# Squares on ScalarE and moved outer products, with attention's first tiles inside the projection and packed scores

## The reference

```
hn   = rmsnorm(x, norm1_g);  proj = hn @ w_in        # 1024 x 2048: q, k, v, u of 512 each
q, k: 4 heads, 2 components of 64;  v: 4 heads of 128
sc   = q . k * 64**-0.5 - slope[h] * |qpos - kpos|   # per head and component
p    = softmax(sc);  a = p[0] - lam * p[1];  att = a @ v
ssm  = bi_s5_glu(u, ...)                             # state space scan, both directions
h    = x + [rmsnorm(att) * 0.2 ; ssm] @ w_out
h    = h + relu(rmsnorm(h) @ w1)**2 @ w2;  y = rmsnorm(h)
```

## Time and profile before

| | |
|---|---|
| median of 3 runs | 2681.01 us (2678.62 to 2682.8) |
| profiled execution, its span | 2681.7 us |
| PE busy | 2562.9 us, 96% |
| DVE busy | 2093.3 us, 78% |
| ACT busy | 1416.5 us, 53% |
| POOL busy | 327.2 us, 12% |
| projection | 0 to about 398 us |
| attention | about 402 to 1006 us |
| state space stage and the rest | 1010 to 2681.7 us |

### The profile page before, as it was taken

One profiled execution on the slowest core, in us unless ns is written; L12 is line 12 of the kernel. 1 busy time (PEld: TensorE's weight loads), 2 busy tenths in 40 slices (PEclk: granted clock), 3 DMA queues, 4 the chain that ended last, 5 costly groups with the idle time before them and its releaser, 6 DMA issues.

```text
span 2681.7 us, 32621 instructions
## 1 busy us (share of the span) xinstructions
PE 2562.9 (96%) x12804; PEld 2155.2 (80%) x12804; DVE 2093.3 (78%) x2074; ACT 1416.5 (53%) x1737; POOL 327.2 (12%) x221
## 2 busy tenths in 40 slices
PE   7998998999999998988989999999999999999998
PEld 5887777999999986766867888888887888888886
DVE  5866638999999976776898877677888886678885
ACT  3276616878787772224444566543334665543334
POOL 6310001101010003320334000000014000000003
PEclk8999998999999999998999999999999999999999
DMA  5356643020204008977565554452234664452221
GB/s 182 111 181 224 221 135 79 25 69 23 72 23 109 24 11 227 267 232 271 186 220 219 220 222 173 173 219 95 94 111 160 247 219 173 173 204 94 94 79 63
DMA packets 162520, 397.17 MB, mean 148 GB/s; under 512 B 29376, under 2 KB 86976, under 8 KB 134592
## 3 DMA queue, kind: packets, MB, share of 16 engines
q1 hardware_dynamic: 145664, 319.06, 35.9%
q10 hardware_dynamic: 16704, 76.03, 7.2%
HBM read 270.79 MB, written 122.16 MB: 147 GB/s over the span
## 4 chain that ended last, share of the span: by engine, by line
PE 44%; DVE 3%; POOL 1%; DMA 1%; issue 1%; ACT 0%; DVEq 0%; SPq 0%; ACTq 0%; POOLq 0%
PE ml_bank L2447 15%; PE ml_bank L2449 15%; PE ml_bank L2448 15%; POOL kp_tabs L2056 1%; DMA kp_low<-hn_s 1%; DVE ml_res L2327 0%; DVE ml_hb L2361 0%; DVE ml_b_split L2258 0%; DVE ml_w_split L2269 0%; DVE ml_res L2347 0%; DVE ml_rinv L2353 0%; PE ml_bank L2455 0%; DMA ml_hb<-h_s 0%; DMA hn_s<-ml_hb 0%; DVE kp_low L2282 0%
## 5 line engine op out<-in xcount | busy, mean ns | idle before, releaser
L2447 PE MATMUL ml_bank<-ml_b_split,ml_w_split 128*128 128x512 f32 x2016 | 788.8, 391 | 10.1 <-issue 9.8
L2448 PE MATMUL ml_bank<-ml_b_split,ml_w_split 128*128 128x512 f32 x2016 | 785.8, 390 | 0.0
L2449 PE MATMUL ml_bank<-ml_b_split,ml_w_split 128*128 128x512 f32 x2016 | 785.7, 390 | 0.0
L2447 PEld LDWEIGHTS ml_bank<-ml_b_split,ml_w_split 128*128 128x128 f32 x2016 | 379.3, 188 | 93.9 <-issue 14.6
L2448 PEld LDWEIGHTS ml_bank<-ml_b_split,ml_w_split 128*128 128x128 f32 x2016 | 379.6, 188 | 79.7 <-issue 1.2
L2449 PEld LDWEIGHTS ml_bank<-ml_b_split,ml_w_split 128*128 128x128 f32 x2016 | 379.4, 188 | 79.2
L2056 POOL TENSOR_TENSOR kp_tabs<-kp_tabs,ml_square 128x512 f32<-128x512 f32 x55 | 144.2, 2622 | 1266.4 <-ACT ml_square L2160 1259.9
L942 ACT ACTIVATE at_e<-at_e,at_neg_top 128x2048 f32<-128x2048 f32 x128 | 256.5, 2004 | 43.8 <-DVE at_neg_top L1027 43.8
L1148 PEld LDWEIGHTS at_pv<-at_v,at_a_t 128*128 128x128 f32 x2048 | 258.3, 192 | 16.4
L2327 DVE TENSOR_TENSOR ml_res<-ml_bank,ml_res 128x2048 f32<-128x2048 f32 x75 | 171.5, 2287 | 118.8 <-PE ml_bank L2449 118.8
L2094 ACT ACTIVATE ml_b_split<-kp_u_t 128x2048 fp32r<-128x2048 f32 x54 | 103.5, 1917 | 298.1 <-PE ml_bank L2449 298.1
(11 more groups left out here) (225 smaller groups left out, 4097.9 us busy)
## 6 DMA issues: line engine op xcount, KB each, us to landing
act_s<-ml_res ACTq DMA_DIRECT2D x32, 1024.0 KB, 4.0
kp_wide<-in_w_stream SPq DMA_DIRECT2D x18, 1024.0 KB, 5.1
kp_bp<-in_w_stream SPq DMA_DIRECT2D x18, 1024.0 KB, 5.5
kp_tabs<-in_w_stream SPq DMA_DIRECT2D x18, 1024.0 KB, 5.9
ml_r<-in_w_stream SPq DMA_DIRECT2D x18, 1024.0 KB, 6.7
tab_s<-kp_tabs ACTq DMA_DIRECT2D x32, 512.0 KB, 2.7
kp_low<-hn_s SPq DMA_DIRECT2D x16, 1024.0 KB, 5.5
kp_u_t<-hn_s SPq DMA_DIRECT2D x16, 1024.0 KB, 4.9
```

What stands on the lines that cost most here:

```text
L2447: pe.matmul(out, w_hi[:, w], b_hi[:, b], start=fresh and kt == 0, stop=False, skip_group_check=True)
L2448: pe.matmul(out, w_hi[:, w], b_lo[:, b], start=False, stop=False, skip_group_check=True)
L2449: last = pe.matmul(out, w_lo[:, w], b_hi[:, b], start=False, stop=kt == 3, skip_group_check=True)
```

## The change

**In the projection.** For the first two tiles of x (`BY_ACT = 2`) ACT takes the squares, one by one between its weight splits and, for the second tile, after the first statistic; POOL only adds them. On PE `stats(0)` stands before group 4 instead of 3. DVE makes the low parts of all eight first weight pieces before it inverts (`invert(0)`), where two came after; ACT splits pieces 6 and 7 ahead of the root. SP loads x's second tile ahead of w's pieces 6 and 7, and `s_bc` behind them. The outer products move from (26, 29, 34, 37, 42, 45, 50, 53) to (26, 29, 32, 35, 41, 44, 49, 52).

**Between projection and attention.** They become one block. Attention's tiles are laid over memory that the projection no longer needs, its PSUM tiles over the eight banks of the projection. Keys are loaded after group 56; then ACT, DVE and POOL make the split keys, the bias and tiles 0 and 1 of q between their work for groups 57 to 63, and PE does the four halves of the scores of tiles 0 and 1 behind groups 60, 61, 62 and 63.

**In attention.** `scores(n, half)` does half the keys for both components: four matmuls of 128 rows with k_hi, then four of 64 rows with k_lo, c = 0 on rows 0 to 63 and c = 1 on rows 64 to 127, alternating. q's halves for c = 1 are swapped for that (low part on rows 0 to 63), k_lo is held once per component, and q's low part is made by POOL. DVE adds c = 0 and c = 1 in turn, the combination is done in two halves, and a transposition waits only for its half. q has two buffers instead of four. The first loads of the next stage are issued one part a tile.

The core of the diff:

```diff
-PREP_OUTERS = (26, 29, 34, 37, 42, 45, 50, 53)
+PREP_OUTERS = (26, 29, 32, 35, 41, 44, 49, 52)
...
+        for x in range(BY_ACT):
+            for k in range(1, KD):
+                pool.wait_ge(squared, KD * x + k + 1)
...
+                pool.tensor_tensor(square_sum[:], square_sum[:], v_out[:, k % 2], ALU.add)\
+                    .then_inc(pool_step if k < KD - 1 else squares_ready, 1)
...
+        split_w(1)
+        squares(0, range(3))
+        split_w(2)
+        squares(0, range(3, 5))
+        for i in range(3, HALF_W):
+            split_w(i)
+            if i < 6:
+                squares(0, range(i + 2, i + 3))
+        stats(0)
+        prep.time_steps(act)
+        squares(1, range(KD))
...
+            if n == NG - 7:
+                prep.all_used(act)
+                attention.k_high(act, 0, range(4))
+            if n == NG - 6:
+                attention.q_high(act, 0)
+                attention.k_high(act, 0, range(4, 8))
...
+            if n == NG - 4:
+                for before in range(NG - 6, NG - 4):
+                    evacuated(pe, before)
+                pe.wait_ge(rms_ready, NTB)
+            if n >= NG - 4:
+                attention.scores(pe, (n - NG + 4) // 2, n % 2)
...
+        for c in range(2):
+            self.wait(pe, self.biased, 4 * n + 2 * half + c - 1)
+            for bank, keys in enumerate(cols):
+                pe.matmul(self.score[:, c, bank * TB:(bank + 1) * TB], self.q_hl[:, n % 2, c], self.k_hi[h % 2][:, c, keys],
+                          start=True, stop=False)
+        for bank, keys in enumerate(cols):
+            for c in range(2):
+                rows = slice(c * DH, (c + 1) * DH)
+                last = pe.matmul(self.score[:, c, bank * TB:(bank + 1) * TB], self.q_hl[rows, n % 2, c],
+                                 self.k_lo[h % 2][rows, keys], start=False, stop=True)
...
+        for n in range(2, NS):
+            a.scores(pe, n, 0)
+            for j in range(2, 4):
+                a.turn(pe, n - 2, j)
+            for j in range(2):
+                a.values(pe, n - 2, j)
+            a.scores(pe, n, 1)
+            for j in range(2, 4):
+                a.values(pe, n - 2, j)
+            for j in range(2):
+                a.turn(pe, n - 1, j)
```

More of the change, by code:

```diff
@@ L301, in sign_matrices @@
         dve.wait_ge(self.bc_loaded, 16)
[L302 removed]
+        dve.wait_ge(self.const_step, 8)
         for i in (1, 2):
@@ new lines, in phase_project, with wait, is_v, qku_index @@
+    block = ctx.enter_context(nc.Block())
+    def wait(eng, sem, value):
+        if value > 0:
+            eng.wait_ge(sem, value)
+    def is_v(n):
+        return n >= SECOND and n % NGROUP < NV
+    def qku_index(n):
+        return n if n < SECOND else SECOND + (n - SECOND) // NGROUP * NV + n % NGROUP - NV
+    def v_index(n):
+        return (n - SECOND) // NGROUP * NV + n % NGROUP
+    def evacuated(eng, n):
+        if n < 0:
+            return
+        if is_v(n):
+            eng.wait_ge(v_evacuated, v_index(n) + 1)
+        else:
+            eng.wait_ge(qku_evacuated, qku_index(n) + 1)
@@ new lines, in fresh_x, with x_freed, w_slot @@
+    def fresh_x(b):
+        return b > 0 and BLOCK_X[b] != BLOCK_X[b - 1]
+    def x_freed(eng, b, k):
+        freed = sum(fresh_x(c) for c in range(b))
+        if k < KD - 1:
+            eng.wait_ge(x_used, freed * (KD - 1) + k + 1)
+        else:
+            eng.wait_ge(group_done, b * NGROUP)
+    w_pieces = w_in.rearrange("(k p) n -> p k n", p=P)
+    x_tiles = x_t.rearrange("(k p) t -> p k t", p=P)
+    def w_slot(i):
+        return slice((i % HALF_W) * P, (i % HALF_W + 1) * P)
+    @block.sync
@@ L779, in phase_attention @@
+    return block, attention
+class Attention:
     NQ = S // P
@@ new lines, in k_high, with k_low @@
+    def k_high(self, act, h, pieces):
+        for i in pieces:
+            c, cols = i // 4, slice(i % 4 * TB, (i % 4 + 1) * TB)
+            if i == 0:
+                act.wait_ge(self.k_loaded, 64 * (h + 1))
+                self.wait(act, self.scores_done, 4 * self.NQ * (h - 1))
+            act.activation(self.k_hi[h % 2][:, c, cols], self.k_raw[:, c, cols], ACT.Copy).then_inc(self.k_hi_ready, 1)
+    def k_low(self, eng, h, i):
+        c, cols = i // 4, slice(i % 4 * TB, (i % 4 + 1) * TB)
+        rows = slice(c * DH, (c + 1) * DH)
+        eng.wait_ge(self.k_hi_ready, 8 * h + i + 1)
+        return eng.tensor_tensor(self.k_lo[h % 2][rows, cols], self.k_raw[rows, c, cols],
+                                 self.k_hi[h % 2][rows, c, cols].bitcast(F32), ALU.subtract)
@@ new lines, in combine, with first_half @@
+    def combine(self, dve, n, half):
+        slot, cols = n % 2, slice(half * self.HALF, (half + 1) * self.HALF)
+        dve.wait_ge(self.coef_step, 2 * n + 2)
+        dve.scalar_tensor_tensor(self.e[:, slot, 0, cols], self.e[:, slot, 1, cols], self.coef[:, 1:2],
+                                 self.e[:, slot, 0, cols], ALU.mult, ALU.add).then_inc(self.combined, 1)
+    def first_half(self, dve, n):
+        for c in range(2):
+            self.add_bias(dve, n, 0, c)
+        self.coefficient(dve, n - 1)
+        self.combine(dve, n - 1, 0)
@@ new lines, in turn, with values @@
+    def turn(self, pe, n, j):
+        if not 0 <= n < self.NS:
+            return
+        if j % 2 == 0:
+            pe.wait_ge(self.combined, 2 * n + j // 2 + 1)
+        self.wait(pe, self.turned_out, 4 * n + j - 1)
+        for i in range(4):
+            kt = 4 * j + i
+            last = pe.transpose(self.turned[:, j % 2, i * P:(i + 1) * P], self.e[:, n % 2, 0, kt * P:(kt + 1) * P], self.ident[:])
+        last.then_inc(self.turned_done, 1)
+    def values(self, pe, n, j):
+        if not 0 <= n < self.NS:
+            return
+        h = n // self.NQ
+        if j == 0:
+            self.wait(pe, self.pv_out, n - 1)
+            if n % self.NQ == 0:
+                pe.wait_ge(self.v_loaded, 64 * (h + 1))
+        pe.wait_ge(self.turned_out, 4 * n + j + 1)
+        for kt in range(4 * j, 4 * j + 4):
+            last = pe.matmul(self.pv[:, n % 2, 0:P], self.a_t[:, n % 2, kt], self.v[h % 2][kt], start=(kt == 0),
+                             stop=(kt == self.NQ - 1))
+        if j == 3:
+            last.then_inc(self.pv_done, 1)
```

1368 lines of the change are left out of this document (674 added, 694 removed).

## The result

The changed kernel takes 2667.18 us (median; 2665.66 to 2670.53) against 2681.91 (2678.62 to 2691.78) for the kernel before on the same chip: ratio 0.9934, 95% interval 0.992 to 0.9948. The forecast was 2627 with a range to 2664: the direction is right, the gain is 14.7 us instead of 53.8, and the time lies 3 us above the range. The profiled execution's span is 2663.5 us, 18.2 less than before's 2681.7; what follows is counted in it.

The account below looks back on a forecast made before the run. PE was taken to bound attention, with DVE close behind. Gains of 46.3 (attention with packed scores and early tiles), 6 (early squares) and 1.5 (outer products) sum to 53.8: 2681.0 - 53.8 = 2627 us, range 2606 to 2664.

Parts of the forecast that it names:

- first scores, wait and clock: First score halves inside the projection: PE waits 3 us for the keys' low part, plus 1 for the clock behind it.
- tile 2's queries, wait and clock: Start of tile 2 in attention: a query load lands in 7.7 us, under a tile, so it costs nothing.
- 61 tiles: Attention from tile 2 to tile 63: 61 tiles at 8.6 us each plus 3.6 us for halving the bias.
- Part 1, packed scores: Attention's scores: k_lo pairs on 64 rows run side by side, switches at 0.16 us each; 8.6 us a tile.
- The sum's own 7.99: PE's time for an attention tile in us, with pairs side by side and changes of array height free.
- The sign that VectorE would be over 95% busy: Attention: DVE over 95% busy was listed among the signs that the forecast is right.
- rival (c): Attention: pairs in sequence, each switch also stopping the next weight load running ahead; 10.15 us a tile, 2722 us; chance 0.06.
- Rival (a): Attention: PE slower with the packed part, 8.9 to 9.2 us a tile, 2645 to 2664 us; chance 0.16.
- Part 2, early tiles: Attention's first two tiles run between the projection's last groups; tile 2 begins at 411.5 us in the old clock.
- Part 3, early squares: Projection's start: the 9.03 us wait for the first statistic goes, groups 6 and 8 come earlier; 6 us gained.
- Part 4, outer products: Projection: moved outer products leave most of the stall before group 40; 1.5 us gained, from -2 to 8.
- (d): Projection's end: early tiles clog it, PE stands 10 us more at groups 58 to 61; 2637 us; chance 0.08.

## Why the prediction was wrong, step by step

Forecast for attention's end: 959.7 in before's clock, less the 7.5 of parts 3 and 4, 952.2. Measured 983.88, 31.7 later. The profiled gain is short by 53.8 - 18.2 = 35.6. Tile 2's first add, forecast at 411.5 - 7.5 = 404.0, came at 417.80, 13.8 late: the first three lines of the table. (The changed kernel's second trace has it at 419.78, so these lines hold to about 2 us.)

| step | forecast | measured | short by |
|---|---|---|---|
| lead when PE wants the first keys | 7.5 | 380.6 - 375.98 = 4.6 | 2.9 |
| first scores, wait and clock | 4 | 6.10 + (2.04 - 1.07) + (1.22 - 0.73) = 7.6 | 3.6 |
| tile 2's queries, wait and clock | 0 | 6.19, and 1.1 by difference | 7.3 |
| 61 tiles | 528.2 | 545.7 | 17.5 |
| tail, by difference | 20 | 20.4 | 0.4 |
| behind attention's end, by difference | 0 | 3.9 | 3.9 |

**Part 1, packed scores**: half of the miss, and a term of mis-sized cost. Right were side by side, PE as the bound (its waits for VectorE from 448 to 980 us are 2.6 us in all), and 1.2 for a halving (61 x (8.946 - 8.88) = 4.0 against 3.6). Wrong was the price of a change of height: I took one emptying, 0.16, as the upper bound. The sum's own 7.99 and the measured 8.88 make it 0.22, the runs 0.18 to 0.23. What was missing shows in the weight loads: these no longer run ahead. PEld's idle time of this kind in the changed kernel; the kernel with all 128 rows has no such row:

```profile
PEld pj_banks L1193 <- issue: 47.2, 128, 0.7
PEld pj_banks L1221 <- issue: 22.6, 62, 0.4
```

That is 0.37 us ahead of each of the 128 low parts (L1193), and as much on the way back, ahead of the values (L1221) that follow a low part. No run parts this from the emptying of the array: the price of a change is measured, its make-up is read from these rows. The sign that VectorE would be over 95% busy did not come either: it is 481.96 of 542 us, 89%. My rival (c) named this mechanism, but priced it only for pairs in sequence; it belonged into the upper bound of the forecast itself. Rival (a), dearer switches and 8.9 to 9.2 us a tile, is what happened, at its lower end.

By the Trainium skill, "TensorEngine Tiling (Array Packing)", Key Properties, a change of mode drains TensorE; these runs agree, in that a change costs 0.18 to 0.23 us in this place, loads included.

**Part 2, early tiles.** The step that failed is the one that looked at the loads: I priced a query load at its landing time, "so nothing", and not at its place in SP's queue. The load of tile 2 stands behind the projection's last store waits in program order, so it could not start before 409.8. My own rule, each queue that a step is moved past, would have found it. The other wait is the keys' low part: between 1.3 and 5 us I took 3, and it was 6.1. The strips beside GpSimd were seen, but set halfway; the earlier trace rows showed only a stretch of 1.23 to 1.75, and the instruction that met the strips here took 4.5 instead of 0.5.

The Trainium skill, "SBUF — State Buffer", SBUF: two separate sides, has GpSimd and a VectorE operation with two SBUF inputs exclude each other for a whole instruction. By it the prediction had the wait at 5, which I weighed and did not take. The run with the strips moved agrees with it (5.02 against 1.00), and so does the run with the squares back (12.39 against 5.38).

The tiles' place itself is right only if the operands are in time: it costs 5.1 us as it stands (8.0 from group 60) and is worth 8.3 repaired (6 to 7 from group 60).

**Part 3, early squares.** 6 forecast; 6.4 at group 8 in the trace (70.06 before, 63.63 after), 5.9 to 8.1 at attention's end by the run without them, which has a slower start of another kind. The points named (1 to 2 us at group 6, group 8 at 65.4) came as 1.6 and 63.63. The account of the first wait fits the rows: the sum of squares was ready at 30.9 (about 32 forecast), and the statistic ran at 33.5 (33.9). What was missed is behind it: group 8 follows a pause of 4.4 us, at a granted clock of 0.80, and takes 8.50 us where the kernel before takes 6.79, so at group 9 only 4.7 of the lead are left.

**Part 4, outer products.** 1.5 forecast, nothing that can be told measured. The mechanism, tables and then the split of x queued behind an outer product that waits for a store, is the one in the trace; the wait at group 40 stayed, at 10.5 us and not at my 8.5. The 1.5 that did not come here, and the part of the lead lost behind group 8, are the first line of the table.

**The range** was too narrow for one reason: each rival was priced with everything else going as forecast. Rival (a), and waits of the early tiles of the size of (d) but at another place, came together.

## What to carry to other kernels

Packing half-height matmuls between full-height work pays two changes of height for each stretch, here 0.18 to 0.23 us each, with weight loads that no longer run ahead: count them against the slots saved before writing it. In this kernel that left 0.11 of 0.83 us a tile. An early start is worth only what its latest operand allows: walk each load's place in its queue, past the waits of stores too. When a helper step is moved out of the way of one deadline, look at the deadline ahead of its new place.

## What the runs showed of the hardware

Four 64-row matmuls, two on either half of the rows, took 0.71 us in the order A B A B and in the order A A B B; all on one half they took 1.12. What lets a later one overtake in the second order, no run here shows.

GpSimd's first four small subtractions in the changed kernel (shortest, median and longest in ns, first and last start):

```profile
L1032 POOL TENSOR_TENSOR at_q_hl<-at_q_raw,at_q_hl x4: 447/451/4497, 371.4 to 382.6; 64x128 fp32r<-64x128 f32 x4
```

One of 64 x 128 elements took 4.5 us where the other three took about 0.45. It was held through both of VectorE's strips, 4.34 us together, and not only through one.

The reverse is in the run with the squares back: VectorE's eight operations that split x, each with two inputs in SBUF, took 12.39 us beside GpSimd's squares and 5.38 us alone.
